# Latent attention with query halves in the column tiles of the value product, and score products ordered by key operand first, query half second

## The reference, cut to what matters

```python
def attend(q, k, v):
    s = jnp.einsum('bqhgd,bkhd->bhgqk', q, k, preferred_element_type=jnp.float32) * (HEAD_DIM ** -0.5)
    p = jax.nn.softmax(s, axis=-1).astype(v.dtype)
    return jnp.einsum('bhgqk,bkhd->bqhgd', p, v)

k_all = jnp.concatenate([kc, kl], axis=1)
v_all = jnp.concatenate([vc, vl], axis=1)
y_lat = merge(blocked_attention(ql, k_all, v_all), gal, fourier_mix(ul, f_gain, w_fmix), gbl)
```

## Time and profile before

| What | us |
|---|---|
| Median of 3 executions | 3846.14 (3846.03 to 3846.5) |
| Profiled execution, from first to last instruction (the span) | 3843.2 |
| The median less the span | 2.9 |
| Latent attention in the span: first coarse score product to its store | 760.2 to 1891.3 |
| TensorE busy over the whole span | 3536.2 (92%) |
| VectorE busy | 2201.5 (57%) |
| GpSimd busy | 1495.5 (39%) |
| ScalarE busy | 1281.6 (33%) |

### The profile page before, as it was taken

One profiled execution on the slowest core, in us unless ns is written; L12 is line 12 of the kernel. 1 busy time (PEld: TensorE's weight loads), 2 busy tenths in 40 slices (PEclk: granted clock), 3 DMA queues, 4 the chain that ended last, 5 costly groups with the idle time before them and its releaser, 6 DMA issues. The chain is left out here.

```text
span 3843.2 us, 51226 instructions
## 1 busy us (share of the span) xinstructions
PE 3536.2 (92%) x17340; PEld 2668.7 (69%) x17340; DVE 2201.5 (57%) x3467; ACT 1281.6 (33%) x2070; POOL 1495.5 (39%) x991
## 2 busy tenths in 40 slices
PE   6999996799999999999679879999999995999798
PEld 4787883456666666666468667888998884887586
DVE  4666634566666666666436565333334443777576
ACT  3422334334444444444220043222223331664300
POOL 1133313357776777776523321000101001444354
PEclk8999997799999999999889989999999997999899
DMA  5244537311111111111255342212211103667553
GB/s 191 91 117 129 140 91 252 119 27 33 42 34 33 33 34 34 41 34 33 73 182 181 112 146 83 71 69 72 67 62 47 58 24 118 213 218 245 210 206 139
DMA packets 313680, 394.25 MB, mean 103 GB/s; under 512 B 81964, under 2 KB 208060, under 8 KB 313360
## 3 DMA queue, kind: packets, MB, share of 16 engines
q1 hardware_dynamic: 281312, 317.34, 26.8%
q10 hardware_dynamic: 21040, 37.43, 3.1%
q0 software_dynamic: 11136, 36.98, 2.4%
HBM read 267.99 MB, written 121.20 MB: 101 GB/s over the span
## 5 line engine op out<-in xcount | busy, mean ns | idle before, releaser
L1182 DVE TENSOR_REDUCE al_mx<-al_sx 128x1 f32<-128x512 f32 (+1 forms) x960 | 562.3, 632 | 268.7 <-PE al_sx L1259 255.3
L235 PE MATMUL pj_acc<-pj_whi,pj_h_hi 128*128 128x512 f32 x1808 | 712.6, 394 | 0.0
L237 PE MATMUL pj_acc<-pj_whi,pj_h_lo 128*128 128x512 f32 x1808 | 706.9, 391 | 0.0
L236 PE MATMUL pj_acc<-pj_wlo,pj_h_hi 128*128 128x512 f32 x1808 | 706.9, 391 | 0.0
L1122 ACT ACTIVATE al_e<-al_st 128x1024 f32<-128x1024 f32 x432 | 442.6, 1025 | 577.8 <-PE al_st L1272 567.0
L637 DVE TENSOR_TENSOR pj_h_lo<-pj_hall,pj_h_hi 128x1024 fp32r<-128x1024 f32 x258 | 378.8, 1469 | 285.6 <-ACT pj_h_hi L516 285.6
L1152 POOL TENSOR_TENSOR al_acc_p<-al_acc_p,al_e 128x1024 f32<-128x1024 f32 x192 | 456.6, 2378 | 20.0 <-POOL al_acc_p L1148 0.4
L583 POOL TENSOR_TENSOR pj_wlo<-pj_wst,pj_whi 128x2048 fp32r<-128x2048 f32 x28 | 128.8, 4600 | 731.2 <-ACT pj_whi L500 731.2
L516 ACT ACTIVATE pj_h_hi<-pj_hall 128x1024 fp32r<-128x1024 f32 x258 | 270.3, 1055 | 419.4 <-PE pj_acc L237 401.6
L1281 PE MATMUL al_acc<-al_e,vres 128*64 128x512 f32 x1728 | 402.5, 601 | 0.0
L237 PEld LDWEIGHTS pj_acc<-pj_whi,pj_h_lo 128*128 128x128 f32 x1808 | 341.2, 189 | 72.0
(11 more groups left out here) (293 smaller groups left out, 5720.9 us busy)
## 6 DMA issues: line engine op xcount, KB each, us to landing
s_proj<-pj_stage SPq DMA_DIRECT2D x162, 256.0 KB, 2.0
pj_wst<-in_w ACTq DMA_DIRECT2D x28, 1024.0 KB
ml_k<-s_proj SPq DMA_DIRECT2D x36, 512.0 KB, 4.2
ml_v<-s_proj SPq DMA_DIRECT2D x36, 512.0 KB, 8.6
mo_in<-s_proj SPq DMA_DIRECT2D x34, 512.0 KB, 6.0
hm_w<-in_ada_w SPq DMA_DIRECT2D x16, 1024.0 KB, 8.9
ml_qt<-s_qt SPq DMA_DIRECT2D x32, 512.0 KB, 6.1
s_h<-ml_h POOLq DMA_DIRECT2D x32, 512.0 KB, 8.0
```

What stands on the lines that cost most here:

```text
L235: nc.tensor.matmul(out, s_hi, m_hi, start=start, stop=False)
L236: nc.tensor.matmul(out, s_hi, m_lo, start=False, stop=False)
L237: return nc.tensor.matmul(out, s_lo, m_hi, start=False, stop=stop)
L1182: V.tensor_reduce(mx[:, x:x + 1], slots[x % NSX][:, 0:spans[x % NS][1]], AX.X, ALU.max).then_inc(sx_max, 1)
```

## The change

The call for the latent tokens goes to a new function, `latent_attention`, with a block of 1024 queries (24 blocks), written out without a loop. The context stage keeps `attention`. In the new function:

- The two column tiles of the value product hold two halves of the queries (512 each) against the same key tile, and accumulate over all 18 key tiles. There are no two partial sums to fold.
- `scores` goes over 18 single key tiles; for each it issues the high key part with query half 0 and half 1, then the low part with half 0 and half 1.
- The denominators become two products of a matrix of ones (128x64) with the summed exponentials, 512 columns each, in the two column tiles; their reciprocal has 512 columns, taken in two instructions of 256; the quotient `on` (512 columns) is turned by four transposes, copied by ScalarE and stored by two DMAs.
- Coarse score products stay 2 + 2 as before, now over j = 0 to 15 of 18; the denominators stand at place 18 and the turn at place 27 of the list of 42 uses of the three slots.
- Additions: 5 on VectorE and 11 on GpSimd, and one to join, for 18 tiles.

```diff
@@ new function, cut @@
+def latent_attention(nc, m, a, s, keep, kres, vres):
...
+    NP, HALVES = NT, 2
+    BLOCKS = LT * P // (HALVES * CH)
+    TOTAL = NQ * BLOCKS
...
+    RING, C = 6, 3
...
+    DEN_AT, TURN_AT, NSX = 18, 27, 3
+    AHEAD, EXTRA = (2,) * 16 + (0, 0), 2
+    ADD_D, ADD_P = (1, 3, 9, 10, 12), (5, 4, 6, 7, 8, 11, 13, 14, 15, 16, 17)
...
+            def row(n):
+                sp.wait_ge(negm_done, n + 1)
...
+                for i in range(QT):
+                    sp.dma_start(qb[HD:HD + 1, n % 2, i * P:(i + 1) * P].bitcast(F32), negm[:, n % 2, i:i + 1].bitcast(F32)).then_inc(row_ld[n % 2], 16)
...
+            for n in range(TOTAL):
+                if n + 2 < TOTAL:
+                    sp.wait_ge(sx_mm, (n + 1) * NX)
+                    load_x(n + 2)
+                if n:
+                    store(n - 1)
+                if n + 1 < TOTAL:
+                    row(n + 1)
+                if n + 2 < TOTAL:
+                    sp.wait_ge(st_mm, (n + 1) * NP)
+                    load(n + 2)
...
+            for n in range(TOTAL):
+                if n:
+                    out(n - 1)
+                for j in range(NP):
+                    weights(n, j)
+                    if j == 11 and n:
+                        result(n - 1, TURN_AT % NSX)
...
+            def norm(n, slot):
+                dve.wait_ge(den_mm, n + 1)
...
+                for i in range(2):
+                    half = slice(i * CH // 2, (i + 1) * CH // 2)
+                    V.reciprocal(rden[:, half], slots[slot][:, half]).then_inc(rden_done, 1)
...
+                V.tensor_tensor(on[:], ot[:, n % 2, :], rden[:], ALU.mult).then_inc(on_done, 1)
...
+            adds = {3: (0,), 6: (1,), 12: (2, 3), 15: (4,)}
+            for n in range(TOTAL):
+                for j, (extra, ahead) in enumerate(items(n)):
+                    some(extra)
+                    for i in adds.get(j, ()):
+                        add(n, i)
+                    some(ahead)
+                    if j == 16 and n + 1 < TOTAL:
+                        bias(n + 1)
...
+            def slot_free(item):
...
+                if kind == "max":
+                    pe.wait_ge(sx_max, b * NX + x + 1)
+                elif kind == "den":
+                    pe.wait_ge(rden_done, 2 * b + 2)
+                else:
+                    pe.wait_ge(o_done, b + 1)
...
+            def scores(n, j):
...
+                if k >= 2:
+                    pe.wait_ge(e_done, k - 1)
+                keys = slice(j * P, (j + 1) * P)
+                for part, rows in ((0, qa), (1, qb)):
+                    for b in range(HALVES):
+                        y = mm(st[k % 2][:, b], kres[:, part * NKV + g, keys], rows[:, p, b * CH:(b + 1) * CH], start=(part == 0), stop=(part == 1))
...
+            def values(n, j):
...
+                for b in range(HALVES):
+                    y = mm(acc[b * HD:(b + 1) * HD], vres[:, j, group_of(n), :], e[:, k % RING, b], start=(j == 0), stop=(j == NP - 1))
...
+            def denominators(n, slot):
+                pe.wait_ge(asum_done, n + 1)
+                for b in range(HALVES):
+                    y = mm(slots[slot][b * HD:(b + 1) * HD], ones[:], asum[:, n % 2, b], start=True, stop=True)
...
+            def turned(n, slot):
+                pe.wait_ge(on_done, n + 1)
+                for i in range(CH // P):
+                    y = nc.tensor.transpose(slots[slot][:, i * P:(i + 1) * P], on[:, i * P:(i + 1) * P], keep["ident"][:])
@@ program @@
-    attention(nc, m, a, s, keep, kres, vres, "al_", CT, 4, LT // 4, NT)
+    latent_attention(nc, m, a, s, keep, kres, vres)
```

207 lines of the change are left out of this document (added).

## The result

The changed kernel takes 3978.47 us (median of four, 3971.16 to 3993.01) against 3846.32 before, 132 us more. The ratio from all executions is 1.0348, with a 95% interval of 1.0323 to 1.0372, so 3.5% slower. 3983 was forecast. The profiled execution has a span of 3969.5 us. From the first coarse score product to the last store, the latent stage lasts 1257.7 us (760.8 to 2018.5) where it lasted 1131.1 (760.2 to 1891.3): 126.6 us more, nearly all of the difference. The stages behind it are as long as before (1951 and 1952 us).

What follows compares the result with a forecast made beforehand. TensorE was taken to bound the latent stage, hardly waiting. Its own work (-46.9 us), four new waits, opening, coarse products leaving the body and end sum to +136.8: 3843.2 to 3980.0, median 2.9 above, 3983 us; range 3885 to 4028.

Steps and rivals of the forecast that it cites:

- Wait A: Place 21 waits for both reciprocals to free the denominators' slot, places 22 and 23 for maxima: 3.8 us a block, +83.6.
- Wait B: Place 30 waits for ScalarE's copy of the turn, queued behind the exponential of j = 11: 1.9 us, 22 blocks, +41.8.
- Wait C: First score product waits for eight row DMAs issued after the last maximum: 1.5 us, 23 times, +34.5.
- Wait D: Score group of j = 17 waits for the exponential of j = 15, no coarse products between: 0.35 us, 24 times, +8.4.
- Opening: Start of the latent stage: 40 coarse products instead of 20, four more row DMAs, a larger first load: +15.5 us.
- End: Stage's tail from denominators to last store: 8.2 us, where 4.25 lay between last fold and store; +4.
- Fold off, denominators and turn on: TensorE's own work: fold removed -84.6 us, denominators and turn added +37.7, together -46.9.
- The falling clock: Rival, chance 0.09: TensorE's clock drops after waits, 4.6 us at the lower level, 2.3 lost a block, 50 more: 4033 us.
- The cheap reciprocal: Rival, chance 0.20: wide reciprocals on VectorE run at 1.04 ns a column, 62 us less: 3921, or 3899 without that wait.
- the faster steps with equal weights: Rival, chance 0.06: score products with the same weights step at 0.213 instead of 0.227 us, 24 less: 3959.
- the faster value pair: Rival, chance 0.05: value pairs with the same weights in both column tiles take 0.227 us, 173 less: 3810.
- the waits are not there: Rival, chance 0.08: the fold's saving comes and no engine is late, -46.9 + 15.4: 3812 us.

Runs made afterwards that it cites:

- e9_best: Changed kernel with denominators at place 21, turn's copy before j = 10, row DMAs in halves, tiles 9 and 10 on GpSimd, reciprocal in its PSUM slot: 3835.02 us.
- e1_den21: Changed kernel with the denominators moved from place 18 to place 21: 3942.51 us.
- e2_copy: Changed kernel with the two reciprocals replaced by copies of the same 256 columns, division left out: 3906.67 us.
- e3_result: Changed kernel with ScalarE's copy of the turned block ahead of the exponential of j = 10 instead of behind that of j = 11: 3974.32 us.
- e5_order: Changed kernel with the order inside a score group undone, query half first and key part second as before: 3974.64 us.
- e10_psum: Changed kernel with denominators at place 21 and the reciprocal written back into its PSUM slot, where the multiplication reads it: 3906.03 us.

## Why the prediction was right

The time came out within 5 us of the forecast, and every term of the sum stands where it was put. The closeness of the number is partly luck, as the paragraphs on wait A and on the clock show. A measured wait in this table is what its steps in the changed kernel's trace last beyond ordinary ones, with the step behind the wait, which is 0.1 us longer (0.335 instead of 0.23 after 1294.72, as after a switch):

| Term | Forecast us | Measured us | From |
|---|---|---|---|
| Wait A, with the falls of the clock | 83.6 | 75.4 | 2.85 in 8 blocks, 3.76 with a fall in 14 |
| Wait B | 41.8 | 41.0 | step of 1.99 instead of 0.23, and 0.11, 22 times |
| Wait C | 34.5 | 30.3 | step of 1.47 instead of 0.23, and 0.08, 23 times |
| Wait D | 8.4 | 11.3 | step of 0.60 instead of 0.23, and 0.10, 24 times |
| Opening | 15.5 | 14.4 | 30.7 after 16.2 |
| Coarse products that leave the body | -4.1 | -4.1 | not measured apart |
| End | 4.0 | 3.2 | last value product to store, 15.3 after 12.1 |
| Fold off, denominators and turn on | -46.9 | -46.9 | steps of each as forecast, below |
| Sum | 136.8 | 124.6 | |
| Stage | | 126.6 | |

*Fold, denominators and turn.* The denominators take 1.01 with the switch out (1316.17 to 1317.18 above), 0.10 more at each side; the turn 0.35 and 0.09 behind it: 1.21 and 0.44 against 1.20 and 0.44. e9_best shows that the saving is real: with the waits gone a period is 44.86 instead of 45.9.

*Wait A* held in place and mechanism; its parts were off. The reciprocal of 256 columns takes 1.726 us (median) against 1.694 worked out from 1, 2 and 4 columns: the straight line holds within 2% over a factor of 64. The term that was mis-sized is the multiplication's wait for GpSimd: 1.2 us were taken from between 0 and 2.4, and it was 0.29 (0.98 less 0.69) in this placement. In e1_den21 it was 1.35. The value between the bounds is a matter of phase. So the wait at place 21 is 2.14 us (forecast 2.2), but what follows it, forecast at 1.6, is 0.39 at place 22 and 0.1 in each of three longer steps: 2.85 in all instead of 3.8, and 21 us too much in the sum. 22 x 3.04 = 67 us of wait A went with the copies of e2_copy, which left 0.35 a block; the two agree with the 75.4 of the table.

*The falling clock*, the rival at 0.09, happened in part: not after every wait and not for 2.3 us of loss, but 0.9 in 14 of 22 blocks. Its 4.6 us at the lower level stand in no run; the records show 3.4. These 13 us are in no term of the sum, and they made up for more than half of the 21 that the multiplication did not take. That is luck: two errors of the prediction partly cancel. A little more of it lies in the execution that was profiled. It was the fastest of the four, 7 us below their median; beside its stage, 126.6 us longer, the forecast of 136.8 is 10 too high.

*Waits B, C and D* are 1.87, 1.32 and 0.47 us with the step behind them; 1.9, 1.5 and 0.35 were forecast. What the prediction did not price is that they are not worth their size one by one. It added up waits of TensorE rightly, and its paragraph on the cover named VectorE's lateness without a number; e3_result shows that VectorE used the time of wait B to catch up. A sum of waits gives the loss; it does not give what the removal of one will bring.

*What is not accounted for* is 2 us of the stage. The longer steps behind the four waits are a cost that the sum had at nothing: some 6 us behind waits B, C and D and 7 at wait A.

*The rivals.* The cheap reciprocal, the faster steps with equal weights and the faster value pair all fell: 1.726 us, 0.23 (e5_order) and 2.73 a group of six pairs. The waits of the last rival, "the waits are not there", are all in the trace. Its time was also added up wrongly: 3846.1 less 46.9 and plus 15.4 is 3815 and not 3812, and 3823 with wait D, which it does not deny.

## What to carry to other kernels

When the bound engine has no slack, write down for every buffer that it reuses what stands between release and reuse on the other engines' queues: each of these waits could be read from the program order and four durations. The exception is a wait for another engine's lock on operands, whose size is a matter of phase. Put long readers of a slot (a reciprocal of 6 ns a column) where the bound engine has a group of work that needs no slot, and take out waits together: the gain of one alone can be nothing while another engine uses it to catch up.

## What the runs showed of the hardware that was not expected

- The granted clock fell to its lower level for 3.4 us after an idle time of 1.98 us in 14 of 22 blocks, and not once in e1_den21 after idle times of 1.67, nor in e10_psum; both have a mean of 1.00 over the body of the stage.
- Two additions of 1024 columns on VectorE took 2.84 or 4.71 us, according to whether they started near the end of an addition of GpSimd or 0.06 us after its start.
- Spelling the loop out (24 blocks without a loop on any engine) had no visible price: value groups and score steps are as long as in the earlier trace rows.
